# One decoder step of two hybrid layers: the prompt state is summed in a spare corner of the output bank

## The reference

```python
x = x + W_out [ SSD(h) | RMSNorm(SWA(h)) ]      # h = RMSNorm(x)
x = x + FFN(RMSNorm(x))                          # layer 0 dense, layer 1 top 2 of 8 experts
```

```python
y_diag = einsum('bcijgr,bcjgrp->bcigrp', decay * cb[..., None], xdt)
states = einsum('bcjgn,bcjgr,bcjgrp->bcgrpn', bc, exp(last - cs), xdt)
y_off  = einsum('bcign,bcgrpn,bcigr->bcigrp', cc, h_prev, exp(cs))
y      = y_diag + y_off                          # then + d_skip * x, times silu(z), grouped norm
```

## Time and profile before

| | |
|---|---|
| median of 3 runs | 1582.1 us (1579.41 to 1583.76) |
| the profiled execution | 1582.1 us, its span 1580.4 us |
| TensorE busy | 1540.6 us |
| VectorE busy | 283.5 us |
| ScalarE busy | 204.8 us |
| GpSimd busy | 131.0 us |
| pair stage of layer 0, L1016 to the last L1051 | about 157 to 202 us from the start |
| pair stage of layer 1 | about 661 to 706 us |
| expert stage | from about 750 us to the end |

### The profile page before, as it was taken

One profiled execution on the slowest core, in us unless ns is written; L12 is line 12 of the kernel. 1 busy time (PEld: TensorE's weight loads), 2 busy tenths in 40 slices (PEclk: granted clock), 3 DMA queues, 4 the chain that ended last, 5 costly groups with the idle time before them and its releaser, 6 DMA issues.

```text
span 1580.4 us, 44446 instructions
## 1 busy us (share of the span) xinstructions
PE 1540.6 (97%) x20574; PEld 1297.8 (82%) x20574; DVE 283.5 (18%) x680; ACT 204.8 (13%) x527; POOL 131.0 (8%) x200
## 2 busy tenths in 40 slices
PE   7999999999999999998999999999999999999998
PEld 5677666666666667766999999999999999999897
DVE  2354620000000245554000000000000000000021
ACT  1245310000000034522000000000000000000000
POOL 4211125000000020212000000000000000000100
PEclk9999999999999999997999999999999999999999
DMA  9933429976333432432999999999999999999991
GB/s 263 247 103 113 126 88 275 333 252 221 111 103 107 120 113 67 122 118 84 335 363 349 360 358 346 363 339 355 349 352 360 356 348 353 348 369 357 344 350 36
DMA packets 199228, 397.39 MB, mean 251 GB/s; under 512 B 13723, under 2 KB 69667, under 8 KB 198889
## 3 DMA queue, kind: packets, MB, share of 16 engines
q1 hardware_dynamic: 180664, 346.26, 64.2%
q0 software_dynamic: 16816, 45.42, 9.6%
q10 hardware_dynamic: 1568, 2.91, 0.6%
HBM read 359.87 MB, written 36.63 MB: 251 GB/s over the span
## 4 chain that ended last, share of the span: by engine, by line
PE 95%; DVE 2%; issue 1%; ACT 1%; DMA 0%; SPq 0%; ACTq 0%; DVEq 0%
PE bank L1300 34%; PE bank L1322 17%; PE bank L1212 13%; PE bank L755 7%; PE bank L1229 6%; PE bank L738 2%; PE bank L1068 2%; PE bank L1051 2%; PE bank L724 1%; PE bank L1023 1%; PE bank L1262 1%; PE bank L1035 1%; PE bank L678 1%; PE bank L709 1%; PE bank L1336 0%
## 5 line engine op out<-in xcount | busy, mean ns | idle before, releaser
L1300 PE MATMUL bank<-arena,ring 128*64 128x108 f32 x11264 | 532.2, 257 | 8.7 <-issue 7.5
L1300 PEld LDWEIGHTS bank<-arena,ring 128*64 128x64 f32 x11264 | 525.1, 137 | 15.6 <-issue 14.0
L1322 PE MATMUL bank<-arena,ring 128*64 128x108 f32 x5632 | 263.3, 256 | 0.4 <-issue 0.4
L1322 PEld LDWEIGHTS bank<-arena,ring 128*64 128x64 f32 x5632 | 261.7, 137 | 1.2 <-issue 0.8
L1212 PE MATMUL bank<-hnT,ring 128*128 128x336 f32 x704 | 199.1, 446 | 1.8 <-DVE hnT L1678 1.8
L1212 PEld LDWEIGHTS bank<-hnT,ring 128*128 128x128 f32 x704 | 133.7, 190 | 67.3 <-issue 2.3
L755 PE MATMUL bank<-hnT,ring 128*128 128x336 f32 x384 | 119.8, 457 | 0.0
L2135 DVE TENSOR_TENSOR arena<-arena,bank 128x432 f32<-128x432 f32 (+1 forms) x48 | 27.2, 567 | 507.6 <-PE bank L1300 507.6
L1229 PE MATMUL bank<-arena,ring 128*128 128x336 f32 x352 | 99.6, 446 | 0.0
L755 PEld LDWEIGHTS bank<-hnT,ring 128*128 128x128 f32 x384 | 70.7, 192 | 34.9 <-issue 6.8
L1229 PEld LDWEIGHTS bank<-arena,ring 128*128 128x128 f32 x352 | 66.9, 190 | 32.6
(11 more groups left out here) (360 smaller groups left out, 1068.7 us busy)
## 6 DMA issues: line engine op xcount, KB each, us to landing
ring<-in_moe_w_gate SPq DMA_DIRECT2D x88, 1024.0 KB, 6.1
ring<-in_moe_w_up SPq DMA_DIRECT2D x88, 1024.0 KB, 6.4
ring<-in_moe_w_down SPq DMA_DIRECT2D x88, 1024.0 KB, 6.0
ring<-in_w_in SPq DMA_DIRECT2D x16, 1024.0 KB, 6.4
ring<-in_w_gate SPq DMA_DIRECT2D x11, 1024.0 KB, 20.8
ring<-in_w_up SPq DMA_DIRECT2D x11, 1024.0 KB, 18.7
xg_rows<-arena POOLq DMA_DIRECT2D x1, 10800.0 KB, 71.0
y_rows<-arena POOLq DMA_DIRECT2D x1, 10800.0 KB, 113.4
```

Source lines behind the costliest of these rows:

```text
L1300: ins = mm(into[rows, SLOTS * fi:SLOTS * fi + SLOTS], weights[:, c, col:col + 64], xg[:, k0 + c, :], start=(k0 + c == 0 and fi == 0), stop ...
L1322: ins = mm(bank[5 + c // 4][rows, SLOTS * (c % 4):SLOTS * (c % 4) + SLOTS], weights[:, col:col + 64], hid[:, f, :], start=(f == 0 and c % ...
```

## The change

The prompt state is no longer summed in bank 4. It goes to columns 336 to 463 of the bank in which the same pair's outputs are made (bank 5 for pairs 0 and 2, bank 6 for 1 and 3). The outputs need columns 0 to 335 of it. VectorE's copy reads the new place. The output matmuls start new sums in the same bank, so they now wait for the copy of their own pair (`pstate_ready`, `n + 1`). The state matmuls of pairs 2 and 3 wait for what was read from the bank two pairs earlier. Two waits of pair 3 go, one on `sstate_ready` and one on `pstate_ready`, which the new wait covers.

```diff
                 def prompt_state(pr):
                     n, g = 4 * l + pr, pr // 2
                     pe.wait_ge(xw_ready, n + 1)
-                    if pr:
-                        pe.wait_ge(pstate_ready, n)
+                    if pr >= 2:
+                        pe.wait_ge(y_ready, 2 * n - 3)
+                        pe.wait_ge(pstate_ready, n - 1)
                     for j, nj in ((0, 128), (1, 128), (2, NP - 256)):
-                        mm(bank[4][:, 0:128], xw[pr % 2][0:nj, j, :], Btok[0:nj, j, 128 * g:128 * g + 128], start=(j == 0), stop=(j == 2))
+                        mm(bank[5 + pr % 2][:, NT:NT + 128], xw[pr % 2][0:nj, j, :], Btok[0:nj, j, 128 * g:128 * g + 128], start=(j == 0), stop=(j == 2))
@@
                 def outputs_of_pair(pr):
                     n = 4 * l + pr
                     Y = bank[5 + pr % 2]
-                    if pr >= 2:
-                        pe.wait_ge(y_ready, 2 * n - 3)
+                    pe.wait_ge(pstate_ready, n + 1)
@@
                     if pr == 3:
-                        pe.wait_ge(sstate_ready, 8 * l + 6)
                         attention_part(4, 3)
                         sample_states(pr, 1)
-                        pe.wait_ge(pstate_ready, 4 * (l + 1))
                         attention_part(5, 4)
@@
-                    v.tensor_copy(pst[n % 2], bank[4][:, 0:128]).then_inc(pstate_ready, 1)
+                    v.tensor_copy(pst[n % 2], bank[5 + pr % 2][:, NT:NT + 128]).then_inc(pstate_ready, 1)
```

## The result

The changed kernel took 1593.05 us (median of 6 runs, 1589.85 to 1595.77) against 1580.76 us of the kernel before beside it (6 runs): a ratio of 1.008, interval 1.0058 to 1.0101. On another chip it was 1.0097, 1.0075 to 1.0118. The direction was forecast. The forecast was 7.6 us; 12 to 15 us were measured. The profiled execution took 1598.2 us, its span 1596.5 us.

The account below looks back on a forecast made before the run. The prediction took TensorE's instruction stream to bound the pair stages. Eight new waits, 3.33 us in layer 0 and 4.25 in layer 1, added 7.6 us to 1582.1, giving 1589.7 us; range 1585.4 to 1593.4.

Parts of the forecast that it names:

- The stage is TensorE's, and what a wait takes there is lost: Pair stages of both layers: TensorE's instruction stream bounds them, so a wait there costs what it waits.
- What is taken away costs nothing: Pair stages: the waits that go or move with bank 4 never held TensorE; gain 0.
- The size of each stall: Output matmuls waiting for their pair's copy, eight times: 3.33 us in layer 0, 4.25 in layer 1.
- The 0.40 us of L996: Layer 1, pair 0: TensorE's present wait for VectorE's L1968 goes, giving back 0.40 of the 2.03 us stall.
- The store that the copies wait for: Copies of pairs 2 and 3 wait for stores of two pairs before, landing 3.9 us after issue; cost 0.
- Rival 1: Later weight-streaming stages repay the delay: 4.25 us back (1585.4) or all 7.6 (1582.1); chance 0.10.
- Rival 2: A longer stall halves TensorE's clock for some 15 us: 7.5 us more, 1597.2 us; chance 0.06.
- Rival 3: Only pairs 0 and 3 stall, where VectorE is late: 5.8 us, 1587.9 us; chance 0.04.
- The bounds: Added stalls in both pair stages total at least 6.2 us and at most 9.3 us.

Follow-up runs that it names:

- early signal and order: Changed kernel with the copy released by the last of its own state matmuls and taken first by VectorE in pairs 0 and 3: ratio 0.9999 to the kernel before.
- fitted idle products: Changed kernel with all waits kept and unused products, sized to the waits, run by TensorE ahead of them: ratio 1.0033 to the kernel before.
- changed kernel again: The changed kernel with no further edit, timed again on another chip against the kernel before: ratio 1.0097.
- wait in all pairs: Kernel before with bank 4 kept and only the new wait of the output matmuls added, in all four pairs: ratio 1.0105.
- wait in pair 3: Kernel before with bank 4 kept and the new wait of the output matmuls added in pair 3 only: ratio 1.0027.
- routing kept busy: Kernel before with unused products, sized to TensorE's three pauses in the routing stage, put into them: ratio 0.9955, 1570.91 us against 1576.47.

## Why the prediction was right or wrong, point by point

**The stage is TensorE's, and what a wait takes there is lost.** Right. The waits of 0.38 us to 2.1 us came at the eight places named.

**What is taken away costs nothing.** Right: with the waits moved off the path (early signal and order) the shared bank gives 0.9999.

**The size of each stall.** Right. With the clock held up, the stages grew by 3.34 and 4.24 us; the forecast was 3.33 and 4.25. The 0.40 us of L996 in layer 1 are in this: the wait for L1968 is gone from the changed kernel's list.

**The store that the copies wait for.** No wait for it is seen in any profile.

**Rival 1, the delay is repaid.** Refuted as the main way: the kernel is slower by more than the waits, and by about the waits plus the clock lost. Only with the fitted idle products is there a hint that part of the 7.6 us comes back.

**Rival 2, the clock falls.** This is the step that failed. I gave it 0.06 and priced one fall at 7.5 us, from the 15 us of the routing stage, and argued from 655 to 660 us, busy for 3.30 of 5 us at a clock of 1.00, that a stretch otherwise full would hold. What the runs showed in its place: behind the wait of 2.1 us the clock was 0.67 in 671 to 674 and 0.50 in 674 to 677, and the timed executions of the changed kernel again lost 8.3 us of clock that the sum had at nothing.

Of the seven profiles with waits of 1.6 us or more in layer 1, six have the low clock in its pair stage; of the six with one in layer 0, three have it there. The other 17 pair stages of the 15 profiles, with shorter waits or none, have none. It stands behind or around such a wait, or, in the changed kernel again and the wait in all pairs, in layer 1 ahead of pair 0 already. A fall cost 3.3 us in layer 0 (54.16 and 54.18 against 50.91), some 1.4 in the wait in pair 3 (3.10 less the wait of 1.7), and 4.9 us for the two falls of the changed kernel in layer 1 (57.22 less 52.30), not 7.5. The profile of the changed kernel thus holds 7.6 + 4.9 = 12.5 us in the two stages. That this is close to the 12.3 us of the timed runs is partly luck, since the profiled execution itself is 16.1 us longer.

I had taken the fall as one unlikely event of 7.5 us; it was several smaller ones, frequent behind long pauses. What makes one pause lower the clock and another not stays open: the wait in pair 3 alone lost no clock in the timed executions, and the short waits of pairs 1 and 2 lost 3.5 us of it. The Trainium skill ("TensorE: Matmul & The Clock Gate", "What's actually happening") says that the lower clock is what TensorE gets unless activity lifts it. The trace agrees in so far as the clock fell in 9 of 13 stages with a long wait and stayed at 1.00 where idle products filled the waits.

**Rival 3, waits only in pairs 0 and 3.** Refuted: pairs 1 and 2 waited 0.38 us each.

**The bounds.** 6.2 to 9.3 us for the waits held (3.34 + 4.24 us); the range for the time took in no fall, so 1593.05 us lies at its upper edge (1593.4) and the ratios of 1.008 and 1.0097 times 1582.1 us (1594.8 and 1597.4) beyond it.

## What to carry to other kernels

Where TensorE is the bound, a copy out of PSUM that its next matmul waits for costs copy plus backlog of the copying engine; released by the last matmul that it needs and taken first on the copying engine, it cost nothing measurable here (0.9999). Count the idle time of such pauses twice: once as time, and once as a chance that the next microseconds run at half the clock (here in 9 of 13 stages with a pause of 1.6 us or more). Where a pause couldn't be removed, idle products that fit in it came with a full clock (1.0033 in the pair stages, 0.9955 in the routing stage); ones that are too long eat the gain (1.0079 and 0.9994). Judge a clock by the timed executions, not by one profile.

## What the runs showed of the hardware that I had not expected

The low clock of 0.50 appears in stretches in which TensorE was busy throughout, too: 0.83 in 530 to 540 of the changed kernel with 10.00 of 10 us busy. Such stretches lie at the same few places in kernels of all kinds (between 20 and 80 us, or about 220, 530 and 580 us, and about 1480 us), in a mix that changes from one execution to the next. The kernel before has them too: the profile of "routing kept busy", whose program is the same up to the routing stage, has those at 220, 530 and 580 us. Whether the change makes them more frequent isn't shown, and they are why one profile alone can't price a fall.

The routing stage of the kernel before had spent some 6 us on the low clock (46.14 against 39.78 us), more than all of the waits in layer 1 cost. The page showed it as one digit, a 7 in the row of the clock.
